# When a decoder step's expert dot products, table-two rows and number turns are made: new places in the projection, the attention and the query stage

## What is computed

```python
q = (xb @ w_q).reshape(TOK_BLK, PEER_HEADS, 2, DK_HALF)
s = jnp.einsum('thcd,hcnd->thcn', q, sub_keys)
s1, i1 = lax.top_k(s[:, :, 0], TOPK)
s2, i2 = lax.top_k(s[:, :, 1], TOPK)
cand = (s1[..., :, None] + s2[..., None, :]).reshape(TOK_BLK, PEER_HEADS, TOPK * TOPK)
cid = (i1[..., :, None] * N_KEYS + i2[..., None, :]).reshape(TOK_BLK, PEER_HEADS, TOPK * TOPK)
top_s, pos = lax.top_k(cand, TOPK)
eid = jnp.take_along_axis(cid, pos, axis=-1)
g = jax.nn.softmax(top_s, axis=-1)
hid = jax.nn.gelu(jnp.einsum('thkd,td->thk', u_tab[eid], xb), approximate=False)
y = jnp.einsum('thk,thkd->td', g * hid, v_tab[eid])
```

## Time and profile before

| | us |
|---|---|
| median of 3 runs | 1928.96 (1928.77 to 1934.21) |
| the profiled execution | 1921.95 |
| its span | 1920.1 |
| busy: PE / DVE / ACT / POOL | 1461.1 / 1088.8 / 215.4 / 1042.8 |
| HBM traffic | 348 GB/s over the span |

### The profile page before, as it was taken

One profiled execution on the slowest core, in us unless ns is written; L12 is line 12 of the kernel. 1 busy time (PEld: TensorE's weight loads), 2 busy tenths in 40 slices (PEclk: granted clock), 3 DMA queues, 4 the chain that ended last, 5 costly groups with the idle time before them and its releaser, 6 DMA issues.

```text
span 1920.1 us, 16500 instructions
## 1 busy us (share of the span) xinstructions
PE 1461.1 (76%) x5398; PEld 535.6 (28%) x5398; DVE 1088.8 (57%) x2879; ACT 215.4 (11%) x610; POOL 1042.8 (54%) x1119
## 2 busy tenths in 40 slices
PE   6889895778879898836267777777676766788997
PEld 3475553435343354401011111111111111111221
DVE  2267987665265625645876666667777776433000
ACT  2321112444200111100100000010000000100000
POOL 3023443222445446647567677776666666676664
PEclk9899997687989899969699999999999999999999
DMA  9588788979989779959899999999999999999997
GB/s 326 177 312 304 282 328 322 339 278 379 332 320 379 296 265 402 388 217 410 318 364 407 399 404 403 389 409 372 373 377 373 375 360 360 373 409 410 372 364 287
DMA packets 213254, 670.00 MB, mean 349 GB/s; under 512 B 19600, under 2 KB 54656, under 8 KB 213040
## 3 DMA queue, kind: packets, MB, share of 16 engines
q0 software_dynamic: 157728, 571.78, 77.5%
q1 hardware_dynamic: 55440, 97.16, 14.2%
HBM read 663.26 MB, written 5.60 MB: 348 GB/s over the span
## 4 chain that ended last, share of the span: by engine, by line
PE 26%; DVE 24%; DMA 23%; POOL 14%; issue 10%; ACT 2%; DVEq 0%; SPq 0%; POOLq 0%; ACTq 0%
POOL area_r L1570 14%; DMA area_r<-in_u_tab,eid 14%; PE bank L769 8%; DMA area_r<-in_v_tab,eidT 8%; DVE area_r L1425 7%; PE bank L715 4%; PE bank L666 3%; PE bank L543 3%; PE bank L627 1%; DMA area_w<-in_w_in 1%; DVE area_w L1354 1%; DVE area_w L1352 1%; DVE rt L1355 1%; PE bank L578 1%; PE bank L613 1%
## 5 line engine op out<-in xcount | busy, mean ns | idle before, releaser
L1425 DVE CUSTOM_DVE_ANT_0 area_r<-area_r,bank 128x1024 f32<-128x1024 f32 x544 | 648.6, 1217 | 419.0 <-DMA area_r<-in_u_tab,eid 418.0
L769 PE MATMUL bank<-area_r,area_c 128*32 128x512 f32 (+1 forms) x1632 | 705.0, 615 | 217.8 <-DMA area_r<-in_v_tab,eidT 217.4
L1570 POOL DMA_INDIRECT area_r<-in_u_tab,eid x544 | 514.3, 945 | 565.1 <-DVE hid L1425 329.3
L1570 POOL DMA_INDIRECT area_r<-in_v_tab,eidT x544 | 513.0, 943 | 297.2 <-PE bank L769 151.2
L769 PEld LDWEIGHTS bank<-area_r,area_c 128*32 128x32 f32 (+1 forms) x1632 | 139.7, 110 | 744.2 <-DMA area_r<-in_v_tab,eidT 483.6
L769 PE MATMUL bank<-area_r,area_v 128*32 128x512 f32 (+1 forms) x544 | 263.3, 607 | 55.9 <-DMA area_r<-in_v_tab,eidT 55.9
L543 PE MATMUL bank<-area_w,area_t 128*128 128x384 f32 (+1 forms) x448 | 159.5, 513 | 5.5 <-DMA area_w<-in_w_in 5.0
L715 PE MATMUL bank<-area_t,area_w 128*128 128x128 f32 (+2 forms) x672 | 126.5, 348 | 5.5 <-ACT area_x L873 3.7
L769 PEld LDWEIGHTS bank<-area_r,area_v 128*32 128x32 f32 (+1 forms) x544 | 48.5, 109 | 221.2 <-DMA area_r<-in_v_tab,eidT 138.0
L715 PEld LDWEIGHTS bank<-area_t,area_w 128*128 128x128 f32 x672 | 97.8, 196 | 35.5 <-issue 25.0
L543 PEld LDWEIGHTS bank<-area_w,area_t 128*128 128x128 f32 x448 | 85.3, 194 | 70.4 <-issue 19.2
(11 more groups left out here) (168 smaller groups left out, 980.5 us busy)
## 6 DMA issues: line engine op xcount, KB each, us to landing
area_w<-in_w_q SPq DMA_DIRECT2D x21, 1024.0 KB, 8.0
area_w<-in_w_in SPq DMA_DIRECT2D x12, 1536.0 KB, 13.4
area_w<-in_k_cache SPq DMA_DIRECT2D x8, 1920.0 KB, 15.3
area_w<-in_v_cache SPq DMA_DIRECT2D x8, 1920.0 KB, 10.7
area_r<-in_u_tab,eid POOLq DMA_INDIRECT x544, 6.9
area_r<-in_v_tab,eidT POOLq DMA_INDIRECT x544, 6.7
area_w<-in_w_out SPq DMA_DIRECT2D x4, 2048.0 KB, 9.8
area_w<-in_w_in SPq DMA_DIRECT2D x2, 2048.0 KB, 15.5
```

The source lines that it names most:

```text
L769: mm = pe.matmul(acc[CG * g:CG * g + m, e, :], wd[g][:, c * CG:c * CG + m], v_ring[s][:, e * 512:(e + 1) * 512], start=False, stop=False, ...
L1425: vec.tensor_tensor_reduce(out=u_ring[s], in0=u_ring[s], in1=x_cur, scale=1.0, scalar=0.0, op0=ALU.mult, op1=ALU.add, accum_out=hid[t % 2] ...
L1570: nc.gpsimd.indirect_dma_start(out=ring[s], out_offset=None, in_=table, in_offset=bass.IndirectOffsetOnAxis(ap=where, axis=0)).then_inc(la ...
```

## The change

Four things are changed, all of them in the order of the work; what is computed stays.

- VectorE makes 68 rather than 84 dots by the end of the projection, and routings 2 to 4 (not 5) stand there. In the attention it makes two dots between a sample's mask and its normalising, one for a pair, and five behind a pair that has a sample next, unless a routing stands there; routings 5, 6 and 7 are in three of those places (steps 1, 4 and 10). That is 59 in the loop; the last dot is made behind it.
- 30 rather than 20 gathers of table two go ahead of tile 1's first gather of table one.
- TensorE weighs 9 + 12 rather than 6 + 8 rows around tile 1's second half of W_out, 4 rather than 3 behind each of the five early query jobs, and in the eight later jobs one row after each half of each product, four for a job, rather than six behind it.
- Before tile 1's numbers are turned, the rows are brought to 112 (before: 101 were done there).

```diff
--- before.py
+++ after.py
@@ -58,19 +58,20 @@
 FIRST = [sum(STEPS[:t]) for t in range(NT)]
 NSTEP = sum(STEPS)
 
-DOTS_FIRST, DOTS_PROJ = 12, 84
-ROUTE_PROJ = {4: 2, 11: 3, 17: 4, 23: 5}
-ROUTE_ATT = {2: 6, 9: 7}
+DOTS_FIRST, DOTS_PROJ = 12, 68
+ROUTE_PROJ = {4: 2, 11: 3, 18: 4}
+ROUTE_ATT = {1: 5, 4: 6, 10: 7}
 ROUTE_STEP = ({g: [g + 2] for g in range(8, 14)} | {15: [16], 16: [17, 18]} | {g: [g + 2] for g in range(17, 24)}
               | {g: [2 * g - 22, 2 * g - 21] for g in range(24, 31)})
 TOPS_ATT = 16
 NORM_AT = {SLOTS + 24: 2, SLOTS + 30: 3, SLOTS + 37: 4}
-V_LEAD = 20
+V_LEAD = 30
 V_BESIDE = 4
-V_PER_EARLY = 3
-V_PER_JOB = 6
+V_PER_EARLY = 4
+V_PER_JOB = 4
 EARLY = 5
 EID_AT = 92
+EID_FIRST = 112
 
 
 def build(nc, x_p, x_s, k_cache, v_cache, gains, w_in, ln_gb, w_sT, b_sT, w_out, w_q, keysT, u_tab, v_tab,
@@ -325,8 +326,16 @@
         def dots_by_unit(u):
             return DOTS_FIRST + (DOTS_PROJ - DOTS_FIRST) * (u - NC + 1) // N_REST_U
 
-        def dots_by_group(i):
-            return DOTS_PROJ + (SLOTS - DOTS_PROJ) * (i - NG0 + 1) // N_ITER
+
+
+        def dots_in_group(i, j):
+            if not NG0 <= i < NG:
+                return 0
+            sample = ATT[GROUP[i][0]][0] == "s"
+            before = i + 1 < NG and ATT[GROUP[i + 1][0]][0] == "s"
+            if j == 0:
+                return 2 if sample else 1
+            return 5 if before and i - NG0 not in ROUTE_ATT else 0
 
 
         JOBS = ([(h, [0]) for h in range(HEADS)] + [(h, [1]) for h in range(EARLY)]
@@ -700,7 +709,7 @@
                     mm.then_inc(xn_turned, 1)
 
 
-            def queries(i):
+            def queries(i, tokens=0):
                 h = JOBS[i][0]
                 a, n = job_tokens(i)
                 w = wq_first[h] if i < HEADS else wq_ring[(i - HEADS) % 3]
@@ -714,7 +723,11 @@
                     for k in range(KD):
                         mm = pe.matmul(half(4 + c)[:, 0:n], w[:, k, c * P:(c + 1) * P], featT[:, k, a:a + n],
                                        start=(k == 0), stop=(k == KD - 1))
+                        if tokens and k == KD // 2 - 1:
+                            weigh_first(tokens // 4)
                     mm.then_inc(q_done[c], 1)
+                    if tokens:
+                        weigh_first(tokens // 4)
 
             def key_scores(i):
                 h, ts = JOBS[i]
@@ -830,8 +843,8 @@
             pe.wait_ge(eidT_ready, 1)
             start_sum(0)
             pe.wait_ge(w_out_again[1], 16)
-            project_out(1, 1, 6)
-            weigh_first(8)
+            project_out(1, 1, 9)
+            weigh_first(12)
             turn_xn(1)
             pe.wait_ge(xnT_ready, 4)
             pe.wait_ge(x2_ready, 4)
@@ -850,12 +863,12 @@
                     turn_xn(t - 1)
             pe.wait_ge(xnT_ready, 2 * NT)
             pe.wait_ge(x2_ready, 2 * NT)
-            queries(EARLY_END)
+            queries(EARLY_END, V_PER_JOB)
             for i in range(EARLY_END, len(JOBS)):
                 if i + 1 < len(JOBS):
-                    queries(i + 1)
+                    queries(i + 1, V_PER_JOB)
                 key_scores(i)
-                weigh_first(V_PER_JOB)
+            weigh_first(max(EID_FIRST - made[0], 0))
             turn_eid(1)
             weigh_first(V_OF[0] - made[0])
             for t in range(1, NT):
@@ -1501,14 +1514,14 @@
                 vec.memset(q_blk[s], 0.0).then_inc(qz, 1)
 
             def experts_between(i, j):
-                if j == 0 and i - NG0 in ROUTE_ATT:
+                if j == 1 and i - NG0 in ROUTE_ATT:
                     route(ROUTE_ATT[i - NG0])
                 if j == 1 and i - NG0 == TOPS_ATT:
                     finish_gates(0)
-                lo, hi = dots_by_group(i - 1), dots_by_group(i)
-                dots_to(lo + (hi - lo + 1) // 2 if j == 0 else hi)
+                dots_to(min(made_dots[0] + dots_in_group(i, j), SLOTS))
 
             attend(NG0, NG, experts_between)
+            dots_to(SLOTS)
             dve.wait_ge(pv_done, len(ATT))
             dve.sem_inc(v_free, VR)
             copy_eidT(0)
```

## The result

The changed kernel takes 1946.3 us (median of 4 runs, 1944.24 to 1947.89) where before takes 1928.87 beside it. The ratio is 1.0087, with a 95% interval of [1.0062, 1.0111] (brackets behind a ratio mean that throughout). The whole interval lies above 1, so the kernel is **slower**, by 0.9%, and past the upper end of the range (1940). Its profiled execution took 1947.89 us (span 1946.1), 25.9 above that of before; by medians it is 17.4.

What follows compares the result with a forecast made beforehand. From 936 us the DMA engines are full, so the end follows GpSimd's gather queue into that stretch: 1929.0, less 7 us by the attention's end, less 0 at tile 1's turn, gives 1922 us; range 1902 to 1940.

Steps and rivals of the forecast that it cites:

- Rows inside the query products: Query stage, 662.7 to 807.7: 145 us with 97 rows done, where before had 101 done at 816.8.
- the early jobs' further rows: Five early query jobs: a fourth row added to three costs TensorE nothing to speak of; four rows 2.03 us, one 1.83.
- the likeliest case: The main forecast, whole kernel: 1922 us, its own range 1912 to 1929, chance 0.36.
- Projection: Projection stage: VectorE loses 28 us of work, TensorE ends 11 us earlier, first mask moves from 314.63 to about 292.4.
- Attention: Attention stage: 73.6 MB at 402 GB/s plus 12 us unused; first table-two gather at 485, 6 us earlier.
- rival (a): Attention transfers stay at 345 GB/s, not 402: first table-two gather at 503, 12 later, kernel 1940; chance 0.24.
- First products of table two: From table two's first gather: tile 1's activations turn 8 us later, mostly hidden; first wide query product 1 us later, 662.7.
- cover of 8.67 us: Last turn of activations: TensorE's old 8.67 us wait for VectorE there hides its 8 to 9 us of lateness.
- rival (b): Query stage takes the gain back: cover used up, wide products at 671, +8 us, 1929; chance 0.24 together with (d), gaps staying.
- Turn of tile 1's numbers: After the query stage, 807.7: turn at 861 with 335 gathers out; even, 0 us, with -5 to +9.
- that sign: At the turn of tile 1's numbers: a state more than 10 gathers from 335 would show the forecast wrong.
- After: Behind the turn of tile 1's numbers: sum of gathers same, 11.00 us wait at 934.35 stays, nothing changes.

Runs made afterwards that it cites:

- c3_after_six: The changed kernel with two more table-two rows behind each later query job's key scores, six a job rather than four: ratio 0.9907 to before.
- a3: The changed kernel with ScalarE's store of the last sample's outputs moved ahead of this sample's exponentials: ratio 1.0045 to before.
- run 4: The kernel before with ScalarE's store of the last sample's outputs moved ahead of this sample's exponentials: ratio 0.9904 to before.
- b1: Before with 30 table-two gathers ahead, 9 + 12 rows around W_out, four per early job, six still behind each later job: ratio 0.9948.
- c1: Before's projection and attention with the change's query part, but six rows a later job, four inside the products and two behind key scores: ratio 0.9910.
- The four kernels of the table: Before's attention, lead of 30; a later job's rows six or four: all behind it 0.9948 and 0.9946, four of them inside 0.9910 and 1.0085.
- the gaining halves of this change: Query-side parts on before: lead of 30 with more early rows, 0.9948; four of six later rows singly inside the products, lead 20, 0.9966.
- a2_query_only: The changed kernel with before's projection and attention, so only the query part of the change: ratio 1.0085 to before.
- two halves: The changed kernel with before's query part, 1.0017, and the changed kernel with before's projection and attention, 1.0085; their product is 1.0102.

## Why the prediction was wrong

The step that failed is the one from 662.7 to 807.7, "Rows inside the query products". It took 97 rows at 807.7 and 101 at 816.8 as even, and added nothing for the wait for ScalarE's copy. The changed stage took 161.1 us for the 145 said and weighed a narrow job's four rows in 18.5 us, where before weighed six in 18.1; with two rows a job put back (c3_after_six) the loss was gone. Ahead of it, a second term was put at next to nothing, the early jobs' further rows, and cost 8.0 us.

In numbers: the likeliest case had tile 1's turn at 861 - 7 = 854; it stood at 887.1. The 33 us come out by its own steps.

**Projection: right.** First mask at 289.94 (292.4 said), with the first scores 14.0 us sooner for 11 said; the 12.7 and 11.2 us of waits are down to 2.7 and 0.5 in the same view of after, 143 to 300 us.

**Attention: 3.5 us late of the 485, near by luck, from two wrong terms.** I took 73.6 MB at 402 GB/s and 12 us unused, 195 us. Measured: 346 GB/s for 198 us, 68.5 MB, as only 54 gathers fell into the stage; 68.5 MB at 402 are 170, so 28 us stayed unused, more than the upper bound of 27. The unused time was one mis-sized term: I went near its low end, "since two of the three routings now stand where K and V for the next sample are already in flight". What the unused time waited for is only in part known: TensorE's wait at the bank that ScalarE's order keeps is in the rows, but its removal (a3) gained 3.4 us. The 346 is rival (a)'s 345, though with fewer bytes it cost far less than (a) said. VectorE's interval of 20.3 us with a routing was close too (308.64 to the next sample mask, 330.37, 21.7). The Trainium skill's 358 GB/s ("DMA: Bandwidth & Descriptors", section "Where 436 GB/s comes from") stands between the stage's 346 and the 371 that run 4 moved with the wait gone: as a ceiling run 4 contradicts it here, where one core ran, and as the stage's rate it was nearer than my 402. In a note just ahead of that section the Trainium skill has about 358 GB/s for each core when both cores of the memory's domain stream. No run here shows that case.

**First products of table two: 11.5 us short.** The turn of activations came 43.1 us behind the first gather instead of 34.6, the 8 us said. But "a fourth to three in the five early jobs costs TensorE nothing to speak of" was wrong: their end went from 577.4 to 592.0, 8.5 us more than the turn's delay (60.4 us from turn to end for 51.9). TensorE's waits for rows did not grow, 10.1 us in two waits before and 10.7 in six after. The weighing itself did, from the turn to the end of these jobs, before and after (stretch, length, busy and count of the weighing's instructions, clock, DMA share, GB/s):

```profile
527.37:578.10 50.73, 19.62 (x60) 0.90 0.88 325
```

```profile
533.40:592.70 59.30, 27.60 (x80) 0.97 0.93 348
```

Five more rows cost 8.0 us. The 2.03 us for four rows holds when they have landed together; a row that lands by itself is weighed by itself, at 1.83 to 1.90 us, and most of the later ones did (573.83, 576.62, 586.83 and 590.17 are single). With VectorE later too the cover of 8.67 us was no cover: 3.54 of wait remained and the wide product began 183.3 us after table two's first gather rather than 170.8. That is rival (b): it named 671 on the old clock, and on that clock, counted from table two's first gather, the product stood at 674.2. That the trace itself reads 671.80 is chance, since it holds the attention's gain. With the attention's 4.6 (488.49 against the 483.9 that the 7 us amount to) it is 16.1 us.

**Rows inside the products: 16.1 us short, and the price of them missed.** 145 us said, 161.1 measured (671.80 to the last key scores at 832.9). In a narrow job a half product with its single row is 3.97 us where I added 3.84. From the end of the last single to the next product it is 2.65 us where I had 1.25 for key scores: 1.81 for the key scores themselves and 0.84 (0.95 in wide jobs) of wait for ScalarE's copy of the queries, which the six rows behind the key scores used to cover. That is 1.9 us a narrow job and 2.0 a wide one, 15 us over the eight. The prediction priced what GpSimd would wait and not this.

**Turn of tile 1's numbers: right in length.** From the stage's end to the turn 53.3 us said, 54.2 measured, though TensorE waited 23.52 us of it and not some 10. 335 gathers were out, as said, but that sign could not fail: the 335 follow from the order of the program, whatever the time. The signs that did fail were the stage's end (800 to 808 said, 832.9) and the attention's DMA share (0.95 said, 0.92). "Even" failed by what came before it. I compared 97 rows at 807.7 with 101 at 816.8 and took them as equal, and overlooked that six rows had cost the old job no more time than four cost the new one. The sum is 16.1 + 16.1 + 0.9 = 33.1 us.

**After.** Nothing changes, as said: 27.6 us at 961.90, 26.0 at the end. And rival (b) was priced at 8 us without the second half of the loss; a rate of rows per stage, compared with GpSimd's 2.48 us, would have priced it.

What stays open: what the new attention waits for once ScalarE's order is out of the way, which of lead and early rows gives b1's gain, and whether c1 is really below b1 (their intervals meet, on different chips). The four kernels of the table ran on three chips, so only their ratios to before beside them are compared.

## What to carry to other kernels

When work is interleaved into a stage that is fed by a queue, compute what the stage consumes **per us**, before and after, and set it against the queue's pace; splitting lengthens the stage, so fewer items in it must not come on top. Work behind a stage's dependent step can be the cover of a short wait: before moving it all away, leave as much as covers it (here two rows, 0.4 to 0.8 us for both). Price work by how it will arrive: four rows together took 2.03 us, four alone 7.3. And before filling one engine's gaps, follow what else stands in order behind the released step on the next engine: moving one store ahead of one exponential brought before to 0.9904, by itself, where the gaining halves of this change brought 0.9948 and 0.9966 (the intervals meet, on different chips). In the changed attention the same move gave next to nothing, so the gap it closes has to be the one that holds the stage.

## What the hardware showed that was not expected

The same stretch of gathers from 1000 to 1200 us, in before on the first chip and in a2_query_only on another:

```profile
1000.00:1200.00 200.00, 145.18 (x307) 27.29 (x305) 132.96 (x325) 1.59 (x2) 144.10 (x153) 1.00 1.02 404
```

```profile
1000.00:1200.00 200.00, 133.89 (x273) 24.77 (x272) 122.35 (x309) 0.00 (x0) 126.50 (x135) 0.97 0.95 356
```

153 gathers against 135, in a code that is the same there: 404 and 356 GB/s. Before takes 1929 us on the one and 2051 to 2053 on the three others. The ratios agree all the same (1.0102 from two halves, 1.0087 for the whole).
